# Norms in and around a recurrent layer: last squares totalled apart, gate totals moved, operands moved to PSUM, and a new order of the beginning

## The reference

```python
mod = c @ w_ada[l] + b_ada[l]
shift, scale, gate = jnp.split(mod, 3, axis=-1)
h = rms_norm(x, g_pre[l]) * (1.0 + scale[:, None, :]) + shift[:, None, :]
proj = h @ w_in[l]
...
x = x + gate[:, None, :] * rms_norm(y, g_post[l])
...
u = _rmsnorm(h, norm_w[i])
h = h + _short_conv_mixer(u, conv_in_w[j], conv_w[j], conv_out_w[j])
...
h = h * lax.rsqrt(jnp.mean(h * h, axis=-1, keepdims=True) + RMS_EPS)
h = h * head_norm_w.astype(jnp.float32).reshape(N_HEADS, DV)
h = h.reshape(bsz, T, E_MLSTM).astype(u.dtype) * jax.nn.sigmoid(o) * jax.nn.silu(z)
return h @ w_out
```

## Time and profile before

| what | value |
|---|---|
| profiled execution, its own time | 1549.52 us |
| its span, first to last instruction | 1547.8 us |
| median of the runs | 1550.52 us |
| TensorE busy | 1491.0 us, 96% |
| VectorE, ACT, GpSimd busy | 737.2, 529.0, 596.6 us |
| mean granted clock | 0.991 |

### The profile page before, as it was taken

The page is one execution under the profiler, slowest core; times in us unless marked ns, Lnnn a source line. Parts: engine busy times, 40 slices in busy tenths (PEclk is TensorE's granted clock), DMA queues, the critical chain, the costliest instruction groups (busy, mean ns, idle before and its releaser), DMA issues.

```text
span 1547.8 us, 24784 instructions
## 1 busy us (share of the span) xinstructions
PE 1491.0 (96%) x9498; PEld 1341.3 (87%) x9498; DVE 737.2 (48%) x1553; ACT 529.0 (34%) x944; POOL 596.6 (39%) x481
## 2 busy tenths in 40 slices
PE   3999999999999999999999999999999999999996
PEld 2788888888877999999999999888798889879875
DVE  6635766667667732433423311433623633362374
ACT  5534344343434323223222222323413332241232
POOL 5563231321355154344343354233443343344331
PEclk9999999999999999999999999999999999999997
DMA  9331111111243132222222222222121132212111
GB/s 382 110 125 66 55 54 54 56 53 55 109 168 131 56 109 82 81 104 85 82 88 85 99 82 86 77 96 90 60 102 68 61 108 81 95 59 104 67 43 55
DMA packets 23635, 140.28 MB, mean 91 GB/s; under 512 B 3352, under 2 KB 3352, under 8 KB 7712
## 3 DMA queue, kind: packets, MB, share of 16 engines
q1 hardware_dynamic: 18320, 127.93, 23.0%
q10 hardware_dynamic: 5264, 11.64, 2.2%
HBM read 137.45 MB, written 2.11 MB: 90 GB/s over the span
## 4 chain that ended last, share of the span: by engine, by line
issue 41%; PE 30%; POOL 23%; DVE 4%; ACT 1%; DMA 1%; POOLq 0%; DVEq 0%; ACTq 0%
PE lin L387 24%; POOL w_lo L328 23%; PE aux L931 3%; PE aux L903 1%; DVE mix L1795 1%; DMA residual<-x_t 1%; DVE square_sum L413 1%; PE aux L449 1%; POOL residual L360 0%; PE aux L912 0%; DVE squares L1813 0%; PE aux L421 0%; DVE tmp L1734 0%; DVE residual L1850 0%; DVE v_T L1791 0%
## 5 line engine op out<-in xcount | busy, mean ns | idle before, releaser
L328 POOL TENSOR_TENSOR w_lo<-w_raw,w_hi 128x512 fp32r<-128x512 f32 x448 | 583.0, 1333 | 918.6 <-ACT w_hi L375 918.6
L387 PE MATMUL lin<-x_hi,w_hi 128*128 128x512 f32 (+2 forms) x2056 | 556.8, 325 | 16.5 <-DVE x_lo L1330 6.9
L387 PE MATMUL lin<-x_lo,w_hi 128*128 128x512 f32 (+2 forms) x2056 | 551.2, 323 | 0.0
L387 PE MATMUL lin<-x_hi,w_lo 128*128 128x512 f32 (+2 forms) x2056 | 548.2, 321 | 0.0
L387 PEld LDWEIGHTS lin<-x_hi,w_hi 128*128 128x128 f32 x2056 | 341.0, 189 | 48.4 <-issue 9.6
L387 PEld LDWEIGHTS lin<-x_hi,w_lo 128*128 128x128 f32 x2056 | 340.9, 189 | 29.9
L387 PEld LDWEIGHTS lin<-x_lo,w_hi 128*128 128x128 f32 x2056 | 341.0, 189 | 25.9
L375 ACT ACTIVATE w_hi<-w_raw 128x1024 fp32r<-128x1024 f32 x224 | 223.8, 1049 | 150.9 <-PE lin L387 145.5
L1047 ACT ACTIVATE prob<-prob,neg_max 128x31 f32<-128x31 f32 (+6 forms) x128 | 60.2, 471 | 132.3 <-DVE neg_max L1458 132.3
L1601 DVE TENSOR_TENSOR conv_in<-conv_c_gate,lin 128x272 f32<-128x272 f32 (+1 forms) x30 | 11.6, 427 | 191.2 <-PE lin L387 191.2
L387 PE MATMUL lin<-mix,w_hi 128*128 128x512 f32 x256 | 81.8, 401 | 2.5 <-DVE mix L1795 1.9
(11 more groups left out here) (327 smaller groups left out, 1892.5 us busy)
## 6 DMA issues: line engine op xcount, KB each, us to landing
w_raw<-wstream SPq DMA_DIRECT2D x112, 1024.0 KB, 4.7
ada_shift_scale<-w_ada SPq DMA_DIRECT2D x8, 1024.0 KB, 20.7
ada_gate<-w_ada_gate ACTq DMA_DIRECT2D x4, 1024.0 KB, 5.5
residual<-x_t SPq DMA_DIRECT2D x1, 2048.0 KB, 10.3
residual<-x_t ACTq DMA_DIRECT2D x1, 2048.0 KB, 8.4
out_t<-residual ACTq DMA_DIRECT2D x8, 256.0 KB, 2.1
neg_m<-row_store ACTq DMA_DIRECT2D x4, 256.0 KB, 3.2
e_m<-row_store ACTq DMA_DIRECT2D x4, 256.0 KB, 3.1
```

What stands on the lines that cost most here:

```text
L328: eng.tensor_tensor(wlo[h][:, cols], raw[h][:, cols], whi[h][:, cols].bitcast(F32), ALU.subtract).then_inc(s_lo, 1)
L387: ins = t.matmul(o, w[half][:, c0:c0 + P], x(k, t0, cnt), start=(n == 0), stop=(n == 3 * kts - 1))
```

## The change

At the beginning x comes in two DMAs (five tiles, three tiles), the first weight chunk behind the first shift-and-scale weights, and c as one row that TensorE spreads with a product by ones. The squares go into eight buffers, six of them in PSUM. TensorE totals the running sum of six squares and the sum of the last two one after the other into the same columns. ACT evaluates a Sqrt on a constant at the start. GpSimd's list interleaves x over rms, low parts of both chunks, and now the low parts of x for tiles 3 to 7; VectorE keeps tiles 0 to 2. TensorE's steps have a new order.

In n1 and n4 the last square isn't added by VectorE; TensorE totals it by itself after the sum of the others. The gate's totals stand in two halves around n1, and so do VectorE's operations on them. `low_u(k - 1)` stands ahead of the addition of tile k.

In the heads hn is totalled and spread by one product of a matrix of ones with `square_sum`; root and reciprocal work on 128x512 in PSUM. `gbuf`, the copied z and the inverse lie in PSUM. A head's mask sums and decays are made within it, after tile 3. In n4 the spread is made twice, into two banks, and GpSimd scales the last two tiles, whose output DMAs SyncE issues.

The diff, cut. Left out are a renamed semaphore in attention, constants of counts, the same replacement of `rstd` or `sq` by a PSUM bank in further tiles, and removed lines of the old loop in `first_projects`.

```diff
 N_ADA, N_GATE = 8, 4
+X_FIRST, LOW_DVE = 5, 3
+N_LAST_POOL = 2
...
 def _(eng):
-    eng.dma_start(res[:, :, META:T2], x_t).then_inc(s_x, 16)
-    eng.dma_start(raw[0][:], wstream[0, :, :]).then_inc(raw_full[0], 16)
+    eng.dma_start(res[:, 0:X_FIRST, META:T2], x_t[:, 0:X_FIRST, :]).then_inc(s_x, 16)
+    eng.dma_start(res[:, X_FIRST:, META:T2], x_t[:, X_FIRST:, :]).then_inc(s_x_rest, 16)
...
-        if k == 4:
-            eng.dma_start(raw[1][:], wstream[1, :, :]).then_inc(raw_full[1], 16)
+        if k in (1, 4):
+            h = k // 4
+            eng.dma_start(raw[h][:], wstream[h, :, :]).then_inc(raw_full[h], 16)
...
+    for k in range(KD - N_LAST_POOL, KD):
+        eng.wait_ge(s_xhat, N_LAST_POOL + k + 1)
+        eng.dma_start(out_t[P * k:P * k + P, :], res[:, k, META:T2]).then_inc(s_out, 16)
...
-    low_parts(0, 0)
+    def x_hat(k):
+        eng.tensor_tensor(res[:, k, META:T2], res[:, k, META:T2], rstd[:, 0:T1], ALU.mult).then_inc(s_xhat, 1)
+    def x_low(k):
+        eng.wait_ge(s_xhi, k + 1)
+        eng.wait_ge(s_xlo, k)
+        eng.tensor_tensor(xlo[:, k, 0:T1], tmp[:, k % 2, 0:T1], xhi[:, k, 0:T1].bitcast(F32), ALU.subtract).then_inc(s_xlo, 1)
+    low_parts(0, 0, pieces=[0])
...
-    for k in range(KD):
-        eng.tensor_tensor(res[:, k, META:T2], res[:, k, META:T2], rstd[:, 0:T1], ALU.mult).then_inc(s_xhat, 1)
-        if 2 <= k < 2 + PIECES:
-            low_parts(1, 1, pieces=[k - 2])
+    for k in range(3):
+        x_hat(k)
+    low_parts(0, 0, pieces=[1])
+    x_hat(3)
+    low_parts(0, 0, pieces=[2])
+    x_hat(4)
+    low_parts(0, 0, pieces=[3])
+    x_hat(5)
+    x_low(3)
+    low_parts(1, 1, pieces=[0])
+    x_hat(6)
+    x_low(4)
+    low_parts(1, 1, pieces=[1])
+    x_hat(7)
+    x_low(5)
+    low_parts(1, 1, pieces=[2])
+    x_low(6)
+    low_parts(1, 1, pieces=[3])
+    x_low(7)
...
+    eng.wait_ge(s_rstd, 2)
+    for k in range(KD - N_LAST_POOL, KD):
+        eng.tensor_tensor(res[:, k, META:T2], res[:, k, META:T2], rstd[:, 0:T1], ALU.mult).then_inc(s_xhat, 1)
...
+def square_bank(k):
+    return sq[:, 1 - k // 6, 0:T1] if k in (0, 6) else aux[k - 1][:] if k < 5 else lin[0][:, k // 7, :]
...
 def total_columns(t, src, tbs, bank_of, first=True, last=True):
-    for j, t0, ln in token_tiles(tbs):
-        ins = t.matmul(bank_of(j)[0:ln, j:j + 1], src[:, t0:t0 + ln], ones[:, 0:1], start=first, stop=last)
+    for n, (j, t0, ln) in enumerate(token_tiles(tbs)):
+        ins = t.matmul(bank_of(j)[0:ln, j:j + 1], src[:, t0:t0 + ln], ones[:, 0:1], start=first and (last or n == 0),
+                       stop=last and (first or ln == P and t0 + ln >= T1))
...
 V_TILES = (V_S, V_W, V_B)
-gbuf = [tmp[:, 1, 0:T1], sq[:, 0, 0:T1]]
+gbuf = [aux[x][:] for x in range(2)]
...
     eng.wait_ge(s_const, 21)
-    norm_total_pe(eng, n0, TB1, KD)
+    eng.wait_ge(s_c, 16)
+    for b in range(2):
+        ins = eng.matmul(c_spread[:, 512 * b:512 * b + 512], ones[0:1, :], c_rows[0:1, 512 * b:512 * b + 512], start=True, stop=True)
+    ins.then_inc(s_mod, 1)
+    eng.wait_ge(n0.added, KD - 3)
+    total_columns(eng, ssum, TB1, lambda j: aux[2], last=False)
+    eng.wait_ge(n0.added, KD - 2)
+    total_columns(eng, sq[:, 0, :], TB1, lambda j: aux[2], first=False).then_inc(n0.total, 1)
...
+        for c, k in ([(0, k) for k in range(4)] + [(1, 0), (0, 4), (1, 1), (1, 2), (0, 5), (1, 3), (1, 4), (0, 6), (1, 5)]
+                     + [(0, 7), (1, 6), (1, 7)]):
+            ready[c](k)
+            if c == 0:
+                eng.wait_ge(s_xlo, k + 1)
+            for g in range(2):
+                ins = group(eng, c, g * P, 256, KD, [(proj_bank(c, g), TB1[0])], x_hi, x_lo, ks=[k])
+                if k == KD - 1:
+                    ins.then_inc(s_chunk if g else s_proj, 1)
...
-    for c in range(N_GATE):
+    def gate_total(c):
...
-            ins = eng.matmul(aux[0][:, 2 * c + j:2 * c + j + 1], gate_acc[:, c, P * j:P * j + P], ones[:, 0:1],
+            ins = eng.matmul(aux[c // 2][:, 2 * c + j:2 * c + j + 1], gate_acc[:, c, P * j:P * j + P], ones[:, 0:1],
...
-    ins.then_inc(s_gate_tot, 1)
-    norm_total_pe(eng, n1, TB1, KD)
+        return ins
+    eng.wait_ge(n1.added, KD - 2)
+    total_columns(eng, ssum, TB1, lambda j: aux[2], last=False)
+    gate_total(0)
+    eng.wait_ge(n1.squared, KD)
+    total_columns(eng, sq[:, (KD - 1) % 2, :], TB1, lambda j: aux[2], first=False).then_inc(n1.total, 1)
+    gate_total(1).then_inc(s_gate_tot, 1)
...
+    gate_total(2)
+    gate_total(3).then_inc(s_gate_tot, 1)
...
         head_projections(ii, (12,))
-        norm_total_pe(eng, hn, TB1, 4, ii)
+        eng.wait_ge(hn.added, ii * 3 + 3)
+        eng.matmul(aux[2][:], ones[:], ssum[:, 0:T1], start=True, stop=True).then_inc(hn.total, 1)
...
-        norm_spread_pe(eng, hn, TB1, ii)
...
     head(LH - 1, True)
-    norm_total_pe(eng, n4, TB1, KD)
+    eng.wait_ge(n4.added, KD - 2)
+    total_columns(eng, ssum, TB1, lambda j: aux[2], last=False)
+    eng.wait_ge(n4.squared, KD)
+    total_columns(eng, sq[:, (KD - 1) % 2, :], TB1, lambda j: aux[2], first=False).then_inc(n4.total, 1)
+    norm_spread_pe(eng, n4, TB1, bank=3)
...
-    eng.dma_start(c_rows[:], c_row).then_inc(s_c, 16)
+    eng.dma_start(c_rows[0:1, :], c_row).then_inc(s_c, 16)
+    eng.wait_ge(s_const, 21)
+    act(rcol[:, 0:1], eps[:], ACT.Sqrt)
...
-        if k >= 2:
-            eng.wait_ge(n0.added, max(k - 2, 1))
-        act(sq[:, k % 2, 0:T1], res[:, k, META:T2], ACT.Square).then_inc(n0.squared, 1)
+        if k == X_FIRST:
+            eng.wait_ge(s_x_rest, 16)
+        act(square_bank(k), res[:, k, META:T2], ACT.Square).then_inc(n0.squared, 1)
+    norm_root_act(eng, n0, TB1, D)
...
-    eng.wait_ge(s_const, 21)
-    norm_root_act(eng, n0, TB1, D)
...
         eng.wait_ge(s_xhat, k + 1)
-        eng.wait_ge(s_mod, k + 1)
+        eng.wait_ge(s_mod, k + 2)
...
-        act(aux[2 + k % 2][:], res[:, k, META:T2], ACT.Identity, **x_mod)
+        act(aux[2 + k % 2][:] if k < LOW_DVE else tmp[:, k % 2, 0:T1], res[:, k, META:T2], ACT.Identity, **x_mod)
...
-        if k == 1:
+        if k == 2:
...
             eng.wait_ge(s_ml_out, ii * 16 + (13 + k))
-            act(sq[:, 1, 0:T1], tmp[:, 0, 0:T1], ACT.Tanh, scale=0.5).then_inc(s_z_ml, 1)
+            act(sq[:, 1, 0:T1], aux[3][:], ACT.Tanh, scale=0.5).then_inc(s_z_ml, 1)
...
+            if c == 1:
+                head_decays(ii)
...
                 gate_tanh(0)
-                norm_root_act(eng, hn, TB1, DV, ii)
+                eng.wait_ge(hn.total, ii + 1)
+                act(aux[2][:], aux[2][:], ACT.Sqrt, bias=eps[:], scale=1.0 / DV).then_inc(hn.root, 1)
...
             chunk_lands_and_splits(eng, START["mlstm"] + 10, ii, 10)
-            head_decays(ii + 1)
...
-    head_decays(0)
...
     norm_root_act(eng, n4, TB1, D)
-    for k in range(KD):
+    eng.wait_ge(n4.squared, KD)
+    for k in range(KD - N_LAST_POOL, KD):
+        act(res[:, k, META:T2], res[:, k, META:T2], ACT.Copy, scale=norm_c[:, 2, k:k + 1])
+    eng.wait_ge(n4.spread, 1)
+    act(rstd[:, 0:T1], aux[3][:], ACT.Copy).then_inc(s_rstd, 1)
+    for k in range(KD - N_LAST_POOL):
...
     own.up(ts(mod[:, 16:24], bada[:, 8:16], 1.0, None, ALU.add))
-    eng.wait_ge(s_c, 16)
-    for b in range(2):
-        own.up(copy(c_spread[:, 512 * b:512 * b + 512], c_rows[:, 512 * b:512 * b + 512]))
-    for k in range(KD):
-        norm_add_dve(eng, n0, k, T1, KD)
-    def shift_and_scale(k):
+    eng.wait_ge(n0.squared, 2)
+    tt(ssum[:, 0:T1], square_bank(0), square_bank(1), ALU.add).then_inc(n0.added, 1)
+    for k in range(2, KD - 2):
+        eng.wait_ge(n0.squared, k + 1)
+        eng.wait_ge(n0.added, k - 1)
+        tt(ssum[:, 0:T1], ssum[:, 0:T1], square_bank(k), ALU.add).then_inc(n0.added, 1)
+    eng.wait_ge(n0.squared, KD)
+    tt(sq[:, 0, 0:T1], square_bank(KD - 2), square_bank(KD - 1), ALU.add).then_inc(n0.added, 1)
+    def shift_and_scale(k, between=None):
...
+            if x and between:
+                between()
...
     own.settle()
-    shift_and_scale(0)
-    norm_invert_dve(eng, n0, TB1)
-    shift_and_scale(1)
-    shift_and_scale(2)
-    low(0)
-    low(1)
-    for k in range(3, KD):
+    eng.wait_ge(s_mod, 1)
+    shift_and_scale(0, lambda: norm_invert_dve(eng, n0, TB1))
+    for k in range(1, KD):
...
-        low(k - 1)
-    low(KD - 1)
+        if k <= LOW_DVE:
+            low(k - 1)
...
         for k in (2 * c, 2 * c + 1):
-            norm_add_dve(eng, n1, k, T1, KD)
-    eng.wait_ge(s_gate_tot, 1)
-    own.up(tt(mod[:, 16:24], aux[0][:, 0:8], bada[:, 16:24], ALU.add))
-    own.settle()
-    own.up(tt(gpost[:], gpost[:], mod[:, 16:24], ALU.mult))
+            if k < KD - 1:
+                norm_add_dve(eng, n1, k, T1, KD)
+    def post_gate(half):
+        ks = slice(4 * half, 4 * half + 4)
+        eng.wait_ge(s_gate_tot, half + 1)
+        own.up(tt(mod[:, 16 + ks.start:16 + ks.stop], aux[half][:, ks], bada[:, 16 + ks.start:16 + ks.stop], ALU.add))
+        own.settle()
```

(43 more changed lines are left out.)

37 lines of the change are left out of this document (14 added, 23 removed).

## The result

| | before | after |
|---|---|---|
| median of the runs, us | 1549.08 (1546.44 to 1550.55) | 1527.41 (1527.02 to 1527.76) |
| profiled execution: its own time, span | 1549.52, 1547.8 | 1527.02, 1525.3 |

The ratio is 0.986, 95% interval 0.985 to 0.988: 21.7 us faster by the medians, 22.5 by the profiled executions. 17.3 was forecast, range 1526 to 1541.

What follows compares the result with a forecast made beforehand. TensorE was busy 96% of the span, so time could come only from gaps, dropped instructions and lower-clock stretches. Terms -5.2 + 0.5 - 2.5 - 4.2 - 4.7 - 1.2 = -17.3 gave 1532.2 profiled, median 1533, range 1526 to 1541.

Steps and rivals of the forecast that it cites:

- rival (c): Whole kernel: clock stays up at the final norm and x lands sooner, -21 us in all, 1529; chance 0.07.
- Beginning: Up to the first gate projection: sooner norm and work shared by three engines start it at 51.4, gain 5.2 us.
- sign of being wrong past 48: Beginning: the forecast is wrong if GpSimd's row of low parts ends past 48 us; expected end 45.1.
- Norm ahead of the convolution layer: Norm before the convolution layer: between -0.2 and +1.0 us, taken as +0.5, later.
- The contention I priced at 0.8: Ahead of the convolution layer: the moved low part, two SBUF inputs, is blocked beside GpSimd's w_lo, +0.8 us.
- First head: Recurrent layer's first head: weights split before the decays removes TensorE's wait for low parts, gain 2.5 us.
- Heads 0 to 2: Recurrent heads: 0.7 us less TensorE work and 0.7 less waiting in each of three heads, gain 4.2.
- Last head: Last recurrent head: g ready 2.8 us sooner and TensorE stays at 2.4 GHz, gain 4.7; 2.8 if the clock falls.
- Final norm: Kernel's end: root 1.15 us sooner, two spreads, VectorE scales six tiles and GpSimd two, gain 1.2.
- the 3.7 for spreads at 2.4 GHz: Final norm: gain 3.7 us instead of 1.2 if the spreads run at 2.4 GHz.
- Rival (a): TensorE at 1.2 GHz in the sparse beginning (2.5) and falling in the last head (2.8): -12.7 us, 1538; chance 0.15.
- (d), the late split: Each head: decays delay ACT's split; at 13.7 us delay TensorE waits 5.5 a head, 22 in all, 1555; chance 0.02.

Runs made afterwards that it cites:

- x_whole: Changed kernel with x in one DMA of 2 MB as before, the rest of the beginning as changed; single 1528.82 us, gate projection at 53.80.
- heads_columns: Changed kernel with the heads' norm totalled into columns and spread by small products again, buffers staying in PSUM; single 1535.38 us, heads 86.79 each.
- heads_sbuf: Changed kernel with VectorE's buffers in the heads (copied z, gbuf, inverse) back in SBUF; single 1538.28 us, heads 87.70 each.
- the second execution: The changed kernel profiled again without an edit; single 1526.68 us, 13.29 from the last output product to the end.
- decays_ahead: Changed kernel with each head's mask sums and decays made ahead of it, as in the kernel before; single 1535.01 us.

## Why the prediction was right, and where its sizes were off

The mechanism held in the beginning, at the first head, in the heads and in the last head. Ahead of the convolution layer and at the end the sizes came near by other ways than forecast. The sum missed by 5.2 us, to the good side, and 3.9 of them (2.32 and 1.57 below) are in terms that it did not have. Both come or go with the program, and no run ties them to the change. Without them the change gave 18.6 where 17.3 was forecast. That the total lies nearest to rival (c)'s 1529 is therefore chance.

- **Beginning**, -4.70 for -5.2. Squares started at 8.12, not 7.1. That is a delay of one to one, as `x_whole` shows, and it alone would have given 52.4; the rest of the row was 0.5 quicker than stepped through. The last wait was at 36.59 (forecast 36.0) and 15.3 us of products followed, as said. GpSimd's last low part ended at 45.2 (forecast 45.1, sign of being wrong past 48). Of the 4.98 at the first product 1.6 to 1.86 is the split of x.
- **Norm ahead of the convolution layer**, +0.76 for +0.5; +0.62 to +0.66 at equal clock. The root did start right behind the table load, the spread 0.1 to 0.2 sooner. What failed is the account of VectorE's row as 2.2 a tile that TensorE would hide: it is 2.17 against 2.07 a tile, and low part 7, not the first one, sets the next total. The contention I priced at 0.8 was there before too (0.93 and 1.24 in two executions, 1.21 to 1.82 after) and is not what costs: the first low part still ends 0.10 to 0.16 sooner at the same clock.
- **Convolution layer**, -2.32 for 0. Open, see below.
- **First head**, -4.38 for -2.5. 2.82 is the gap and its restart (143.24 to 140.42, the stretch of executions with the half clock at 989 but without the gap), 1.57 the stretch at half clock, which comes or goes with the program: 7 of 14 executions have it, and the two of each kernel agree. The forecast had no term for it.
- **Heads 0 to 2**, -5.51 for -4.2: 1.84 each for 1.4. The one product was priced rightly (0.86 for 0.9), the small ones 0.2 too low, so TensorE's part is 0.90 (`heads_columns`). The wait of 0.69 cost 0.94 with the restart behind it (87.73 less 86.79). `heads_sbuf` shows that without operands in PSUM nothing would be left of either: the large reciprocal makes VectorE's chain longer, and a wait of 1.55 stands there. The contention went as priced, down to the one operation that still meets GpSimd's (1.39).
- **Last head**, -4.93 for -4.7, and the clock stayed up, as said. `heads_sbuf` brought both waits and the half clock back together.
- **Final norm**, -1.42 for -1.2, near by luck and for the wrong reason. 0.35 is the change at equal clock; the rest is that total and spreads fell into less half clock. The step that failed is "VectorE starts ... 0.2 later than now, and scales six tiles": the saving arrived at VectorE, but the end hangs on the first store, 6.74 to 6.79 us before the last one's landing, and not on VectorE's last tile. For the same reason the 3.7 for spreads at 2.4 GHz did not come: with both spreads at 2.4 GHz the second execution won 1.87 (15.16 less 13.29).

Rival (a) did not come about in the last head, nor in the beginning, where the clock rose at 27.4; (c), "clock stays up at the final norm, x lands sooner", came nearest in size, with x landing later. (d), the late split, shows nowhere: in `decays_ahead` heads take the same 85.89.

## What to carry to other kernels

When a chain over four engines is shortened, look for the engine whose row per tile grows: here the last tile came to set the end, not the first. Moving an operand to PSUM is worth most where a second engine reads SBUF, and it can be what makes another trade pay (here one large reciprocal instead of a wait for the spread and a copy). At a kernel's end look at the first store before the last tile: where the transfers fill the DMA engines, only an earlier first store shortens it. Before a difference of one or two us is put down to an edit, compare the granted clock of both executions at that place, and run each kernel a second time.
